# Eight experts in a two-layer diffusion backbone: 96 token slots and plain fp32 in four 32-column groups instead of 128 slots in split fp32r

## What is computed

```python
logits = (x @ w_router).astype(jnp.float32)          # x: 256 tokens x 1024
top_v, top_i = lax.top_k(logits, TOP_K)              # TOP_K = 2
top_w = jax.nn.softmax(top_v, axis=-1)
gates = jnp.sum(one_hot(top_i, 8) * top_w[..., None], axis=1)
for e in range(8):                                   # 1024 -> 3584 -> 1024
    y = y + gates[:, e:e+1] * ((silu(x @ we_gate[e]) * (x @ we_up[e])) @ we_down[e])
```

## Time and profile before

| | us |
|---|---|
| median of three runs | 1605.54 (1604.23 to 1608.98) |
| the profiled execution | 1617.21 |
| its span, first to last instruction | 1615.4 |
| PE, DVE, ACT busy in it | 1531.6, 1133.4, 977.0 |
| mean granted TensorE clock | 0.953 of 2.4 GHz |

### The profile page before, as it was taken

One profiled execution on the slowest core, in us unless ns is written; L12 is line 12 of the kernel. 1 busy time (PEld: TensorE's weight loads), 2 busy tenths in 40 slices (PEclk: granted clock), 3 DMA queues, 4 the chain that ended last, 5 costly groups with the idle time before them and its releaser, 6 DMA issues.

```text
span 1615.4 us, 23144 instructions
## 1 busy us (share of the span) xinstructions
PE 1531.6 (95%) x8380; PEld 1282.7 (79%) x8380; DVE 1133.4 (70%) x1260; ACT 977.0 (60%) x1131; POOL 30.5 (2%) x62
## 2 busy tenths in 40 slices
PE   7798699999797899999999999999999999999996
PEld 4755689999784878888888888888888888888885
DVE  1431634444514489989988989889989989988893
ACT  1422543344414367768777777777777777877771
POOL 0030000000030000000000000000000000000000
PEclk7898799999797899999999999999999999999997
DMA  9564567777543369989989989989989999998960
GB/s 346 196 215 141 176 242 274 275 275 247 176 158 110 116 227 361 365 327 360 363 326 357 373 316 365 365 317 359 369 313 375 365 337 345 363 371 312 363 247 28
DMA packets 210286, 464.99 MB, mean 288 GB/s; under 512 B 9226, under 2 KB 51892, under 8 KB 195892
## 3 DMA queue, kind: packets, MB, share of 16 engines
q1 hardware_dynamic: 208324, 462.80, 79.2%
q10 hardware_dynamic: 1904, 1.41, 0.3%
HBM read 462.80 MB, written 1.38 MB: 287 GB/s over the span
## 4 chain that ended last, share of the span: by engine, by line
PE 93%; DVE 4%; ACT 2%; issue 1%; DMA 0%; SPq 0%; DVEq 0%; ACTq 0%
PE ps L1515 13%; PE ps L1517 13%; PE ps L1516 13%; PE ps L1536 6%; PE ps L1538 6%; PE ps L1537 6%; PE ps L1272 5%; PE ps L1273 4%; PE ps L1274 4%; PE ps L1237 3%; PE ps L1482 2%; PE ps L1473 2%; PE ps L1283 2%; PE ps L1525 2%; PE ps L1215 1%; PE ps L1247 1%
## 5 line engine op out<-in xcount | busy, mean ns | idle before, releaser
L1036 DVE TENSOR_TENSOR low<-ring,high 128x1024 fp32r<-128x1024 f32 x672 | 795.5, 1222 | 78.4 <-ACT high L732 55.0
L732 ACT ACTIVATE high<-ring 128x1024 fp32r<-128x1024 f32 x672 | 697.5, 1061 | 163.3 <-PE ps L1517 105.1
L1515 PE MATMUL ps<-high,xg 128*128 128x512 f32 x896 | 358.7, 400 | 0.0
L1517 PE MATMUL ps<-high,xg 128*128 128x512 f32 x896 | 351.4, 392 | 0.0
L1516 PE MATMUL ps<-low,xg 128*128 128x512 f32 x896 | 348.2, 389 | 0.0
L828 DVE TENSOR_TENSOR low<-ring,high 128x1024 fp32r<-128x1024 f32 x102 | 121.2, 1222 | 153.1 <-ACT high L582 153.1
L1272 PE MATMUL ps<-hx,high 128*128 128x256 f32 x640 | 184.0, 288 | 28.9 <-DVE hx L869 13.5
L1517 PEld LDWEIGHTS ps<-high,xg 128*128 128x128 f32 x896 | 168.2, 188 | 39.4
L1516 PEld LDWEIGHTS ps<-low,xg 128*128 128x128 f32 x896 | 168.4, 188 | 35.5
L1515 PEld LDWEIGHTS ps<-high,xg 128*128 128x128 f32 x896 | 169.1, 189 | 32.1
L1273 PE MATMUL ps<-hx,high 128*128 128x256 f32 x640 | 182.0, 284 | 0.0
(11 more groups left out here) (200 smaller groups left out, 1294.5 us busy)
## 6 DMA issues: line engine op xcount, KB each, us to landing
ring<-in_moe_w_gate SPq DMA_DIRECT2D x112, 1024.0 KB, 7.1
ring<-in_moe_w_up SPq DMA_DIRECT2D x112, 1024.0 KB, 7.4
ring<-in_moe_w_down SPq DMA_DIRECT2D x112, 1024.0 KB, 6.9
ring<-in_w_ada SPq DMA_DIRECT2D x48, 1024.0 KB, 11.5
ring<-in_ffn_w_gate SPq DMA_DIRECT2D x11, 1024.0 KB, 10.0
ring<-in_ffn_w_up SPq DMA_DIRECT2D x11, 1024.0 KB, 5.4
ring<-in_ffn_w_down SPq DMA_DIRECT2D x11, 1024.0 KB, 7.2
ring<-in_w_in SPq DMA_DIRECT2D x8, 1024.0 KB, 9.6
```

The source lines that it names most:

```text
L732: A(high[:, (MP0 + i) % PIECES, :], ring[:, s, half * PIECE:(half + 1) * PIECE], ACT.Copy).then_inc(high_ready, 1)
L1036: V.tensor_tensor(low[:, q, :], ring[:, n % SLOTS, half * PIECE:(half + 1) * PIECE], high[:, q, :], ALU.subtract).then_inc(low_ready, 1)
L1515: mm(ps[:, bank, :], xh, hi[:, j, :], start=kk == 0, stop=False)
L1517: last = mm(ps[:, bank, :], xl, hi[:, j, :], start=False, stop=kk == KD - 1)
```

## The change

Nothing ahead of the experts' stage is changed, except that the experts' arrays lie elsewhere. In the stage:

- 96 slots (`CAP`) for each expert, and further rounds only if one expert had more.
- No split: `high`, `low`, `split_e` and the fp32r parts of `xg` and of the hidden values are gone. PE reads the weights as they landed. Their place and the ring's make one ring of 14 slots of 1 MB (`ering`), whose slots PE itself sets free (`pieces_used`).
- Plain fp32 matmuls with 32 stationary columns. A *unit* is 32 slots by one block of 512 columns. Gate and up have two blocks of columns in a step (1024 hidden columns, last step 2 x 256) and three groups of slots: twelve units, four in each of banks 0, 1 and 2, on partitions 0, 32, 64 and 96.
- Three steps of 1024 hidden columns and one of 512. An expert has 42 items (28 of gate and up together, 14 of down), and each takes twelve matmuls of 512 columns (24 of 256 in the last step's gate and up).
- Down's row pairs: even and odd hidden rows go to different units, so `Y` is the sum of two. ACT reads the even ones; the new `add_Y` on DVE moves one of them and adds the six odd ones.
- Down of step s - 1 is woven into gate and up of step s, one item after every two (after every one in the last step). The transposes of step 0 come right after `combine` and its addition; `gather` of the next expert comes after the last `turn`.

The diff, cut to its core:

```diff
+CAP = 96
+ROUNDS = -(-N2 // CAP)
...
+E_WIDTH = (512, 512, 512, 256)
+E_COL = (0, 1024, 2048, 3072)
+NSTEP = len(E_WIDTH)
+assert sum(2 * w for w in E_WIDTH) == FE
+
+UNITS = (tuple((0, u, u) for u in range(4)), tuple((1, u, u) for u in range(4)), ((0, 4, 0), (0, 5, 1), (1, 4, 2), (1, 5, 3)))
+
+DOWN = ((0, 0, 0, 3, 0), (0, 0, 1, 3, 1), (0, 0, 2, 3, 2), (0, 1, 2, 3, 3),
+        (0, 1, 0, 4, 0), (0, 1, 1, 4, 1), (1, 0, 2, 4, 2), (1, 0, 1, 4, 3),
+        (1, 0, 0, 5, 0), (1, 1, 1, 5, 1), (1, 1, 2, 5, 2), (1, 1, 0, 5, 3))
+TURN_BANK, GATHER_BANK = 6, 0
+COMBINE_BANKS = (6, 7, 3, 4)
...
+def expert_items():
+
+    def gate_up(s):
+        return [("gu", s, j) for j in range(KD * E_WIDTH[s] // 512)]
+
+    def down(s):
+        return [("d", s, i) for i in range(2 * E_WIDTH[s] // 256)]
+
+    out = gate_up(0)
+    for s in range(1, NSTEP):
+        gu, d = gate_up(s), down(s - 1)
+        each = len(gu) // len(d)
+        for i in range(len(d)):
+            out += gu[each * i:each * (i + 1)] + [d[i]]
+    return out + down(NSTEP - 1)
...
+        ering = nc.alloc_sbuf_tensor_at("ering", [128, ESLOTS, SLOT], f32, offset=ring_at)
...
+                what, s, j = EXPERT[i]
+                width = E_WIDTH[s]
+                arrives = in_slot[E_SLOT[i]]
+                to = ering[:, E_SLOT[i], :]
                 one = slice(e, e + 1) if isinstance(e, int) else bass.ds(e, 1)
                 if what == "d":
-                    r = EC // 128 // 2
-                    src = e_down[one, c, :, half * r:(half + 1) * r, :].rearrange("o p r n -> (o p) r n")
-                    sp.dma_start(slot(i, r, D), src).then_inc(s, 16)
+                    src = e_down[one, E_COL[s] // 256 + j, :, :, :].rearrange("o p r n -> (o p) r n")
+                    sp.dma_start(to.rearrange("p (r n) -> p r n", r=2), src).then_inc(arrives, 16)
                 else:
-                    k = KD // 2
-                    src = (e_gate if what == "g" else e_up)[one, :, half * k:(half + 1) * k, c * EC:(c + 1) * EC].rearrange("o p k n -> (o p) k n")
-                    sp.dma_start(slot(i, k, EC), src).then_inc(s, 16)
+                    k = 512 // width
+                    for half, w in enumerate((e_gate, e_up)):
+                        src = w[one, :, j * k:(j + 1) * k, E_COL[s]:E_COL[s] + 2 * width].rearrange("o p k n -> (o p) k n")
+                        sp.dma_start(to[:, half * SLOT // 2:(half + 1) * SLOT // 2].rearrange("p (k n) -> p k n", k=k), src).then_inc(arrives, 16)
...
-            def split_e(k, a, z):
-
-                for i in range(a, z):
-                    n, half = divmod(i, 2)
-                    s = n % SLOTS
-                    if half == 0:
-                        act.wait_ge(in_slot[s], k * (16 * PER_EXPERT[s]) + (MOE_ARRIVED[s] + 16 * (n // SLOTS + 1)))
-
-                    act.wait_ge(pieces_used, k * E_PIECES + (MP0 + i - PIECES + 1))
-                    A(high[:, (MP0 + i) % PIECES, :], ring[:, s, half * PIECE:(half + 1) * PIECE], ACT.Copy).then_inc(high_ready, 1)
-
...
             def take_Y():
-                A(Y[:, 0:512], ps[:, 4, :], ACT.Copy)
-                A(Y[:, 512:1024], ps[:, 5, :], ACT.Copy).then_inc(Y_ready, 1)
+
+                A(Y[0:CAP, 0:512], ps[0:CAP, 3, :], ACT.Copy)
+                A(Y[0:64, 512:1024], ps[0:64, 4, :], ACT.Copy).then_inc(Y_even_ready, 1)
 
...
+                    for s, width in enumerate(E_WIDTH):
+                        act.wait_ge(pieces_used, k * E_ITEMS + (MP0 + GATE_UP_END[s]))
+                        A(sg[:, 0, 0:width], ps[:, 0, 0:width], ACT.Silu)
+                        A(sg[0:64, 1, 0:width], ps[0:64, 2, 0:width], ACT.Silu).then_inc(esg_ready, 1)
+                        act.wait_ge(ehT_done, k * NSTEP + (s + 1))
+                        n = width // 128
+                        A(hT_first[:, 0:n, :], ps[:, TURN_BANK, 0:width].rearrange("p (n t) -> p n t", n=n), ACT.Copy).then_inc(ehT_first_ready, 1)
 
...
+            def add_Y(n):
+
+                dve.wait_ge(Y_even_ready, n)
+                V.tensor_copy(Y[64:96, 512:1024], ps[96:128, 3, :]).then_inc(Y_moved, 1)
+                dve.wait_ge(Y_moved, n)
+                for odd, half, g, bank, j in DOWN:
+                    if odd:
+                        y = Y[32 * g:32 * g + 32, 512 * half:512 * (half + 1)]
+                        last = V.tensor_tensor(y, ps[32 * j:32 * j + 32, bank, :], y, ALU.add)
+                last.then_inc(Y_ready, 1)
...
+                    add_Y(k + (rnd + 1))
+                    for s, width in enumerate(E_WIDTH):
+                        dve.wait_ge(esg_ready, k * NSTEP + (s + 2))
+                        V.tensor_tensor(hm[:, 0, 0:width], sg[:, 0, 0:width], ps[:, 1, 0:width], ALU.mult)
+                        V.tensor_tensor(hm[0:64, 1, 0:width], sg[0:64, 1, 0:width], ps[64:128, 2, 0:width], ALU.mult).then_inc(eh_ready, 1)
...
+                    def gate_up(s, j):
+
+                        i = E_ITEM["gu", s, j]
+                        width = E_WIDTH[s]
+                        rows = 512 // width
+                        w = arrived_e(i).rearrange("p (t r n) -> p t r n", t=2, r=rows)
+                        for r in range(rows):
+                            kk = j * rows + r
+                            for bank, units in enumerate(UNITS):
+                                for t, u, group in units:
+                                    c, g = divmod(u, 3)
+                                    last = mm(ps[32 * group:32 * group + 32, bank, 0:width], xg[:, kk, 32 * g:32 * g + 32], w[:, t, r, c * width:(c + 1) * width],
+                                              start=kk == 0, stop=kk == KD - 1)
+                        last.then_inc(pieces_used, 1)
+
+                    def turn(s):
+
+                        width = E_WIDTH[s]
+                        pe.wait_ge(eh_ready, k * NSTEP + (s + 1))
+                        for n in range(width // 128):
+
+                            a = n // 2 * 256 + n % 2
+                            nc.tensor.transpose(ps[:, TURN_BANK, n * 128:(n + 1) * 128], hm[:, 0, a:a + 255:2], ident)
+                            last = nc.tensor.transpose(ps[:, TURN_BANK + 1, n * 64:(n + 1) * 64], hm[0:64, 1, a:a + 255:2], ident[0:64, 0:64])
                         last.then_inc(ehT_done, 1)
 
+                    def down(s, i):
+
+                        w = arrived_e(E_ITEM["d", s, i]).rearrange("p (r n) -> p r n", r=2)
+                        c, n = divmod(i, E_WIDTH[s] // 256)
+                        if i == 0:
+                            pe.wait_ge(ehT_first_ready, k * NSTEP + (s + 1))
+                            pe.wait_ge(ehT_last_ready, k * NSTEP + (s + 1))
+                        for odd, half, g, bank, group in DOWN:
+                            u = 3 * c + g
+                            h = (hT_first[:, 2 * n + odd, 32 * u:32 * u + 32] if u < 4 else hT_last[:, 2 * n + odd, 32 * (u - 4):32 * (u - 4) + 32])
+                            last = mm(ps[32 * group:32 * group + 32, bank, :], h, w[:, odd, 512 * half:512 * (half + 1)],
+                                      start=(s, i) == (0, 0), stop=(s, i) == (NSTEP - 1, 2 * E_WIDTH[s] // 256 - 1))
+                        last.then_inc(pieces_used, 1)
+
+                    wait_xg(k + (rnd + 1))
+                    for i, (what, s, j) in enumerate(EXPERT):
+                        if what == "gu":
+                            gate_up(s, j)
+                        else:
+                            down(s, j)
+                        if i + 1 == GATE_UP_END[0]:
+                            pe.wait_ge(Y_ready, k + (rnd + 1))
+                            combine(e)
                             pe.wait_ge(acc_ready, k * 4 + (4 * rnd + 4))
+                            turn(0)
+                        elif what == "d" and s < NSTEP - 1 and j == 2 * E_WIDTH[s] // 256 - 1:
+                            turn(s + 1)
+                            if s + 1 == NSTEP - 1:
+                                gather(e + 1)
```

More of the change, by code:

```diff
@@ L47 @@
 FSTEPS = FF // FC
-EC = 512
-ESTEPS = FE // EC
 SLOTS = 7
@@ L495, in experts @@
                 rest(NE - 1, rnd)
[L497 to L501, removed]
+            for i in range(E_FIRST):
+                if E_SLOT[i] < SLOTS:
+                    n = MOE0 + E_SLOT[i] - SLOTS
+                    if n >= N0:
+                        n -= SLOTS
+                    free(sp, n)
+                else:
+                    sp.wait_ge(pieces_used, MP0)
                 load(0, i)
@@ L506, in _ @@
             with sp.If(more > 0):
-                first_of_next(0, NE - 1)
-                experts(1)
+                for rnd in range(1, ROUNDS):
+                    first_of_next(0, NE * rnd - 1)
+                    experts(rnd)
             sp.wait_ge(y_first_ready, 1)
@@ L763, in experts @@
                 for i in (0, 1):
[L764 removed]
```

(18 more changed lines are left out.)

224 lines of the change are left out of this document (65 added, 159 removed).

## The result

| | before | changed |
|---|---|---|
| median, us | 1605.06 (1604.23 to 1608.98, 4 runs) | 1638.63 (1634.61 to 1641.62, 4 runs) |
| ratio | | 1.020 (95% interval 1.017 to 1.024) |
| span of the profiled execution | 1615.4 | 1632.8 |
| one expert, combine to combine | 125.8 | 128.8 |

The median rose by 33.6 us where 31.6 less was forecast. The two profiled spans differ by only 17.4: in the profile of before, the experts' stage began at 579.7 us, in that of after at 569.6, through work ahead of it that the change doesn't touch: over the first 546 us the granted clock was 0.89 in the one and 0.92 in the other. Two runs of versions further down took 2229 and 2583 us, at mean clocks of 0.64 and 0.55 where the others had 0.94 to 0.96, and are left out of the times given there.

The account below looks back on a forecast made before the run. PE was taken to bound the kernel: an expert's pieces sum to 121.3 us against 125.8, 36 less over eight, 4.4 more at the tail, 1605.5 - 31.6 = 1574 us. Forecast range 1560 to 1588 (0.64); eight in ten 1560 to 1610.

Parts of the forecast that it names:

- waves: Experts' matmuls on PE: 252 groups of four records side by side, 0.430 us each, 108.4 us an expert against 115.4.
- excursions: Going in and out of column groups on PE: 0.23 us each, four times an expert, 0.9 us.
- the waits at steps 1 and 2: PE waiting for silus and products not covered by one item of down: 0.1 us each, 0.2 an expert.
- wait at step 0: PE waiting for the four additions behind combine before the first transposes: 1.5 us an expert, bounds 0 and 2.5.
- tail: After the last expert, `add_Y` (one move, six adds, a hand-over) stands before combine: 4.4 us more.
- what stays: Per expert on PE: combine 3.45 us, transposes 3.3 (28 as before, 14 with 64 moving columns), gather 3.57.
- Rival A: Experts' column-group matmuls can't be fed: 0.446 to 0.470 us per four records, time 1607 to 1655; chance 0.13.
- 79% rule: Skill's three column groups reach 79% of full: 0.544 us per four records, expert 29 us longer, time 1804; chance 0.02.
- B: DMA becomes the bound: halved weight transfers draw only 340 GB/s, about +25 us, 1599; chance 0.06.
- E: A second round in the experts' stage: with 50 to 77 tokens in 96 slots none runs; chance 0.
- C: More small waits in the experts: durations add up end to end, an expert 3.0 us longer, +24, 1598; chance 0.13.
- D: Clock: 1.2 GHz granted over long fp32 stretches, the experts' stage would nearly double; chance 0.02.

## Why the prediction was wrong

The forecast missed by 65 us (31.6 less, 33.6 more). Its steps, by the trace of after (the rows of an expert from the one at 720.3 to 847.6 us, which has no dip):

| step | forecast | measured | miss over the stage, us |
|---|---|---|---|
| waves, 252 an expert, with excursions and the waits at steps 1 and 2 | 108.4 + 0.9 + 0.2 = 109.5 | 109.1 (0.432 or less a wave) | 8 x -0.4 = -3 |
| combine and gather | 3.45 + 3.57 | 3.72 + 3.74 | 8 x 0.44 = 4 |
| transposes, 28 an expert | 3.3 | 8.0 | 8 x 4.7 = 38 |
| wait at step 0 | 1.5 | 1.55 | 0 |
| branch between experts | not in the sum | 1.2 to 1.8 | 7 x 1.4 = 10 |
| clock | "little" | 5 dips of 3.4 us, one of 6.8 | 23.8 us at half speed, so half of it lost: 12 |
| tail | 4.4 more | 5.0 more, combine 5.80 for 3.72 | 3 |

That makes 64. From its first matmul to the end of the last combine the stage takes 1041.4 us in the profile of after and 1011.6 in that of before, so 29.8 more where 31.6 less was forecast: a miss of 61. The table is 3 over it; the medians' 65 hold what lies ahead of the stage and the runs' spread as well. The dips are counted as the profile has them; a run has them in other experts or lengths, so this row is the least certain. The periods bear it out: the two experts behind whose combine the clock held took 127.3 and 127.4 us, the others 129 to 130.

**The step that failed first** is the one on what stays: "Transposes: 28 as before, 14 with 64 moving columns; I leave 3.3." I had counted the transposes and looked at their size, not at their kind. The diff says `hm[0:64, ...]` and `ident[0:64, 0:64]`: that is another shape, and the code alternates it with the full one, eight transposes a turn. I had even priced such a change of shape, for the column groups, at 0.23 an excursion from the earlier trace rows, and then applied it only where the change speaks of column groups: four excursions, where the transposes have 24 more switches. 24 x 0.17 = 4.1 us of the 4.7. Undoing it alone gave 41 us back, some 33 by the switches and the rest by the five dips that went along.

The trace of before held a warning that I overlooked. In the scores of the latent attention fp32 matmuls with 128 and with 64 stationary rows alternate, two records of each; here the first four have 256 moving columns alike:

```profile
115.48 0.70 PE L1362 MATMUL ps<-hid,arena 128*128 128x256 f32 x2
116.11 0.70 PE L1363 MATMUL ps<-arena 64*128 64x256 f32 x2
116.73 0.49 PE L1362 MATMUL ps<-hid,arena 128*128 128x128 f32 x2
```

Two records of 256 columns take 0.63 and 0.62 from start to start here, at a granted clock of 1.00, and 0.43 in combine: 0.2 more for each change. That points to the number of rows, and not that of moving columns, as what counts; no run varied it.

**Rival A**, waves that can't be fed, was my main slower case, and it was the wrong one: it gave 1607 to 1655 and the time falls among them by another mechanism; that it falls there is chance. Waves stayed at 0.43 over stretches of seventy and more. The 79% rule fell with it: four groups side by side bring four times the work in the experts too. B did not show either: 367 GB/s were drawn without a wait, above the 350 that the kernel before had asked for. E did not occur.

**C** was right in kind: small waits and hand-overs. It held neither the switch nor the branch.

**D** I gave 0.02, by "PE has no gap over 1.5 us". The earlier trace rows should have warned me: they showed the clock low over a block of adaLN matmuls in which PE was busy all the time, so the absence of gaps was no safeguard. Combine, the wait and the transposes were never adjacent before the change, and it is at this stretch that the dips came. The wait was worth twice its length for that: undoing 1.2 us of it took 2.4 us off an expert.

**The branch** could not be read from a row of before, where it takes 0.2 us. A hint was there: in fp32 the profile has two records an instruction, so the body would double.

**What was right**: with the three causes removed an expert takes 120.7 us with the loop written out, against a forecast sum of 121.3, and 1574 us, 33 under the kernel before, were reached where 31.6 under it was forecast. That the two agree so well is in part luck: this version waits 0.3 us at step 0 where the forecast had 1.5, and with the wait put back it would be at 121.9. The change's idea was sound and its accounting in the matmuls exact; the loss lay in three places that each took an edit of a line or two.

## What to carry to other kernels

When a change puts matmuls of another shape between others, count the switches of shape in the instruction order and not only the instructions: here 0.17 us each, more than a transpose itself. Sort by shape, or pad the small ones to the common shape, even at the price of more work. Look at what a change makes adjacent: short matmuls, a wait and transposes that were spread became a stretch at which the clock fell here, and then a microsecond of waiting cost two. And when a loop's body grows, look at the branch on the sequencer and at the instruction bytes: it was free here only as long as what was queued covered it, and small matmuls side by side cover less time.

## What was not expected of the hardware

- A switch between a 128x128 transpose and one of 64 rows costs 0.17 us; transposes of one shape come 0.12 apart behind the first, of either size.
- A loop's branch back took 0.21 us with a body of 580 matmul records (an expert of the kernel before), 3.4 us with 1180 (an expert of the changed kernel) and 3.5 us with 1160 (two experts of the kernel before), each with as many weight loads.
- The clock fell to 1.2 GHz for 3.4 us, at times 6.8, in or behind stretches of 6.4 to 8.0 us with combine, a wait and transposes: not at all at 5.2 us, in 0 to 5 experts of 8 at 6.4 to 6.6, in 6 and 8 above, though PE was never idle there for over 1.6 us.
- What was queued on PE when a branch began was 20 matmul records of four column groups, 2.05 us, or 17 of full width, 3.8 us.
- Four fp32 matmuls of 32 stationary columns each run in the time of one of 128 for as long as they are fed: 0.43 us for four records side by side (each matmul has two), with DMA at 367 GB/s beside it.
